# Splitting the weights on GpSimd: two instructions of 1024 columns in place of four of 512

## The chip, the cores and the metric

The kernel runs on one core of a Trainium2 chip. The metric is the time of the whole program on the device in microseconds; the median over several executions counts. In the profile, PE is TensorE's matmul side, DVE is VectorE, ACT is ScalarE, POOL is GpSimd and SP the queue that issues the weights' DMAs.

## The reference

Two networks in a row over one sequence of 512 tokens with 1024 features, all in float32. The first block joins multi-head latent attention and a bidirectional gated linear attention (GLA) behind one input projection, then a gated feed-forward network with a depthwise convolution over the grid. The second block has four layers: a mixer (recurrent, spatial gating, short convolution, recurrent again), each followed by an MLP of width 4096.

```python
def first_block(x, c, ctx, ...):
    mod = jax.nn.silu(c) @ w_ada + b_ada            # shifts, scales and gates from the condition
    h = modulate(rms_norm(x, norm1_g), sh1, sc1);  hc = modulate(rms_norm(ctx, norm1_g), sh1c, sc1c)
    x = x + gt1 * token_mixer(h, hc, ...)           # MLA attention and GLA
    x = x + gt2 * conv_ffn(modulate(rms_norm(x, norm2_g), sh2, sc2), ...)
    return rms_norm(x, final_g)

def second_block(x, ...):
    for i in range(4):
        x = x + mixer[i % 3](_rmsnorm(x, norm_mix_g[i]), ...)
        x = x + _sqrelu_mlp(_rmsnorm(x, norm_mlp_g[i]), mlp_w1[i], mlp_w2[i])
    return _rmsnorm(x, final_norm_g)
```

## The kernel before

Activations lie transposed, 128 features by 512 tokens in a tile, eight tiles for 1024 features. Every weight comes from HBM as a panel of eight 128x128 tiles (128 partitions by 1024 columns, 512 KB); there are 513 panels, and SP loads them into four slots `w_raw`. For accuracy each product is made of three matmuls: weights and activations are split into a high part, rounded to the matmul's format, and a low part, the difference. PE adds high by high, high by low and low by high (`mm`, line 1549), 24 matmuls of 512 columns in a panel.

GpSimd does nothing but split the weights. For a panel, `high(slot)` copies `w_raw` to `w_hi` with rounding (lines 1500 and 1501, the two halves of 512 columns), and `low_then_high` subtracts `w_hi` from `w_raw` into `w_lo` (lines 1511 and 1512, two halves again) and then makes `w_hi` of the next panel. Before `w_lo` of panel n it waits for three things: the next panel's landing, the high part, and `panel_used`, by which PE tells that it has begun panel n-2. So GpSimd runs up to three panels ahead of PE and each of its steps (low of n, high of n+1) is released by PE's first matmul of a panel. `panel_made` follows the second half of `w_lo` and is what PE and SP wait for.

The activations are split by ACT (the high part) and DVE (the low part, a subtraction of two SBUF tensors). Places that the prediction speaks of: `modulated` (lines 1094 and 1098) makes the first norm of `x` (`h_lo`) and of the context (`hc_lo`); `ada_product` (line 1117) multiplies a 128x1024 tile of `w_ada` by the condition vector and sums it, with 14 of these between the norm of `x` and that of the context; in the GLA `decays` (lines 1208, 1210 and 1213: a gated sum, a scan, a difference, each 768 columns wide) precede the transposes on PE; line 1301 adds the rotated half of a query head; line 1444 makes the last low part at the end of the first block, and line 1930 that at the end of each mixer and MLP (`feed_low`, behind the sums of squares of line 1923), always for tile 0 to 7, as PE's next product wants them in this order; line 1994 works on the recurrent mixer's input. Tiles named `acc`, `side` and `stat` are PSUM, all others that count here SBUF. The order of instructions on each engine is that of the program; nothing is scheduled.

Of the kernel before, what the change touches and what calls it, by code (L numbers as in the profile page):

```python
# [18 lines left out]
F32 = mybir.dt.float32  # L19
F32R = mybir.dt.float32r  # L20
ALU = mybir.AluOpType
# [3 lines left out]
P = 128  # L25
# [8 lines left out]
TP = 8  # L34
# [131 lines left out]
def build(nc, io, names, upto=None, start_x=False):  # L166

    n_panels = io["weights"].shape[0]
    with ExitStack() as whole:
        def sem(name):  # L170
            return whole.enter_context(nc.semaphore(name))

        def sb(name, shape, dt=F32):
            return whole.enter_context(nc.sbuf_tensor(name, shape, dt))
# [5 lines left out]
        w_raw = sb("w_raw", [P, SLOTS, TP * P])  # L180
        w_hi = sb("w_hi", [P, SLOTS, TP * P], F32R)
        w_lo = sb("w_lo", [P, SLOTS, TP * P], F32R)
# [41 lines left out]
        hi_made = sem("hi_made")  # L224
# [1241 lines left out]
        @block.sync  # L1466
        def _(sp):
            sp.dma_start(table[:, :], io["table"]).then_inc(const_in, 16)
            sp.dma_start(ones[:, :], io["ones"]).then_inc(const_in, 16)
            sp.dma_start(sgu_mask[:, :], io["sgu_mask"]).then_inc(const_in, 16)  # L1470
            if start_x:
                for k in range(KT):
                    sp.dma_start(x[:, k, :], io["x"][:, k, :]).then_inc(x_in, 16)
            if start_x:
                for slot in range(SLOTS):
                    load_panel(sp, slot, slot)
            if not start_x:
                first_block_sp(sp, load_panel)
            lead = SLOTS if start_x else LEAD
            turns = (n_panels - lead) // SLOTS  # L1480
            with sp.Fori(0, turns) as it:
                for slot in range(SLOTS):

                    sp.wait_ge(panel_made, it * SLOTS + (lead - SLOTS + slot + 1))
                    load_panel(sp, slot, it * SLOTS + (lead + slot))
            for n in range(lead + SLOTS * turns, n_panels):
                sp.wait_ge(panel_made, n - SLOTS + 1)
                load_panel(sp, n % SLOTS, n)
            for k in range(KT):
                sp.wait_ge(scaled, k + 1)  # L1490
                sp.dma_start(io["out"][:, k, :], x[:, k, :]).then_inc(result_out, 16)
            sp.wait_ge(result_out, 16 * KT)


        @block.gpsimd
        def _(pool):
            half = TP * P // 2

            def high(slot):
                pool.tensor_scalar(w_hi[:, slot, 0:half], w_raw[:, slot, 0:half], 1.0, 1.0, ALU.mult, ALU.mult)  # L1500
                pool.tensor_scalar(w_hi[:, slot, half:], w_raw[:, slot, half:], 1.0, 1.0, ALU.mult, ALU.mult).then_inc(hi_made, 1)  # L1501

            def low_then_high(slot, made, landed, used):

                after = (slot + 1) % SLOTS
                if landed is not None:
                    pool.wait_ge(raw_in[after], landed)
                if used is not None:
                    pool.wait_ge(panel_used, used)
                pool.wait_ge(hi_made, made)  # L1510
                pool.tensor_tensor(w_lo[:, slot, 0:half], w_raw[:, slot, 0:half], w_hi[:, slot, 0:half].bitcast(F32), ALU.subtract)  # L1511
                pool.tensor_tensor(w_lo[:, slot, half:], w_raw[:, slot, half:], w_hi[:, slot, half:].bitcast(F32),  # L1512
                                   ALU.subtract).then_inc(panel_made, 1)
                if landed is not None:
                    high(after)

            pool.wait_ge(raw_in[0], 16)
            high(0)
            for n in range(SLOTS - 1):
                low_then_high(n, n + 1, 16, None)  # L1520
            first = SLOTS - 1
            turns = (n_panels - 1 - first) // SLOTS
            with pool.Fori(0, turns) as it:
                for j in range(SLOTS):
                    low_then_high((first + j) % SLOTS, it * SLOTS + (first + j + 1), it * 16 + 32, it * SLOTS + (j + 1))
            for n in range(first + SLOTS * turns, n_panels):
                last = n == n_panels - 1
                low_then_high(n % SLOTS, n + 1, None if last else 16 * ((n + 1) // SLOTS + 1), None if last else n + 2 - SLOTS)
# [917 lines left out]
```

## Time and profile before

| | |
|---|---|
| median of 3 runs | 3238.98 us (3237.74 to 3240.68) |
| the profiled execution | 3237.74 us, its span 3235.8 us |
| PE busy | 3096.5 us, 96% of the span |
| GpSimd busy | 2073.4 us, 64%, 2056 instructions |
| DVE busy | 1455.3 us, 45% |
| ACT busy | 709.3 us, 22% |
| granted TensorE clock, mean | 0.979 |
| chain that ended last | PE 88%, DVE 8%, ACT 2% |

Busy time says which engine has the most work. The chain follows the last instruction back through what released it, so an engine off it has slack at that place. From 0 to 540 us (first block up to the merge of its two branches) PE has many gaps; after that it is busy nearly without one, apart from a few at the ends of stages. An instruction's duration in the profile runs from its issue to its end, so a wait inside the engine for something that no semaphore tells of is part of it.

### The profile page before, as it was taken

Reading aid. Unit: us, or ns where it says so; the run is one execution under the profiler, and the core shown is the slowest. Engines: PE = TensorE matmul, PEld = TensorE weight load, DVE = VectorE, ACT = ScalarE, POOL = GpSimd, SP = SyncE. Lnnn points to the kernel's source line nnn. Section 1 sums busy time; section 2 is a strip of 40 time slices with the busy share of each in tenths; the row PEclk is TensorE's granted clock in tenths of the full one; section 3 lists DMA queues with packets and bytes.
Section 4 is the critical chain, followed back from the end, with each engine's and each line's share of the span. In section 5 each row is a group of like instructions: output and inputs, shape, how many; then the busy total and the mean of one; then the engine's idle time right before and its main releaser. Section 6 shows DMA issues by size and latency. Waiting matters only on the chain.

```text
span 3235.8 us, 38599 instructions
## 1 busy us (share of the span) xinstructions
PE 3096.5 (96%) x13568; PEld 2485.2 (77%) x13568; DVE 1455.3 (45%) x1907; ACT 709.3 (22%) x1203; POOL 2073.4 (64%) x2056
## 2 busy tenths in 40 slices
PE   5878799989999999999999999999999999999998
PEld 3757646868888788888878888888888887888886
DVE  7866763247733774422225422255432226542222
ACT  3245463111000362200022200110211114421110
POOL 4623203756666677777767777777777776777774
PEclk8989899999999999999999999999999999999999
DMA  6701102223222232222232222222222222323221
GB/s 250 248 27 40 33 1 75 95 78 98 98 91 98 85 104 93 96 98 97 93 102 85 98 98 96 93 97 98 92 97 98 98 92 97 104 92 97 98 98 65
DMA packets 86009, 306.68 MB, mean 95 GB/s; under 512 B 9552, under 2 KB 10064, under 8 KB 85632
## 3 DMA queue, kind: packets, MB, share of 16 engines
q1 hardware_dynamic: 82512, 297.73, 27.5%
q10 hardware_dynamic: 3376, 7.24, 0.6%
q8 instruction: 87, 1.43, 0.2%
q14 instruction: 34, 0.28, 0.0%
HBM read 302.84 MB, written 2.10 MB: 94 GB/s over the span
## 4 chain that ended last, share of the span: by engine, by line
PE 88%; DVE 8%; ACT 2%; issue 1%; SPq 1%; DMA 1%; ACTq 0%; DVEq 0%
PE acc L1549 83%; PE side L735 1%; DVE rec_rec_x L1972 1%; PE acc L713 1%; DVE state L1265 1%; DVE ada_more L1117 1%; DMA xc<-in_ctx 1%; SPq L505 1%; PE acc L639 0%; PE acc L606 0%; PE acc L621 0%; PE side L1549 0%; PE stat L1612 0%; PE side L723 0%; DVE prob L1327 0%
## 5 line engine op out<-in xcount | busy, mean ns | idle before, releaser
L1511 POOL TENSOR_TENSOR w_lo<-w_raw,w_hi 128x512 fp32r<-128x512 f32 x513 | 672.2, 1310 | 1094.2 <-PE acc L1549 1067.9
L1549 PE MATMUL acc<-h_hi,w_hi 128*128 128x512 f32 x2224 | 878.7, 395 | 44.4 <-DVE state L1265 14.2
L1549 PE MATMUL acc<-h_lo,w_hi 128*128 128x512 f32 x2224 | 871.5, 392 | 0.0
L1549 PE MATMUL acc<-h_hi,w_lo 128*128 128x512 f32 x2224 | 871.5, 392 | 0.0
L1512 POOL TENSOR_TENSOR w_lo<-w_raw,w_hi 128x512 fp32r<-128x512 f32 x513 | 710.8, 1385 | 0.0
L1549 PEld LDWEIGHTS acc<-h_hi,w_hi 128*128 128x128 f32 x2224 | 420.5, 189 | 145.0 <-DVE state L1265 15.4
L1549 PEld LDWEIGHTS acc<-h_hi,w_lo 128*128 128x128 f32 x2224 | 420.9, 189 | 86.0
L1549 PEld LDWEIGHTS acc<-h_lo,w_hi 128*128 128x128 f32 x2224 | 420.9, 189 | 85.7 <-issue 1.7
L1500 POOL TENSOR_SCALAR w_hi<-w_raw 128x512 fp32r<-128x512 f32 x513 | 406.6, 793 | 37.3 <-DMA w_raw<-in_weights 37.3
L1941 DVE TENSOR_TENSOR x<-acc,x 128x512 f32 (+1 forms) x160 | 110.7, 692 | 671.1 <-PE acc L1549 671.0
L1549 PE MATMUL acc<-mlp_hid_hi,w_hi 128*128 128x512 f32 x1024 | 403.5, 394 | 0.0
L1549 PE MATMUL acc<-mlp_hid_hi,w_lo 128*128 128x512 f32 x1024 | 401.4, 392 | 0.0
L1549 PE MATMUL acc<-mlp_hid_lo,w_hi 128*128 128x512 f32 x1024 | 397.4, 388 | 0.0
L1501 POOL TENSOR_SCALAR w_hi<-w_raw 128x512 fp32r<-128x512 f32 x513 | 341.3, 665 | 0.0
L1869 ACT ACTIVATE mlp_hidden<-mlp_relu 128x512 f32<-128x512 f32 x128 | 81.0, 632 | 884.2 <-DVE mlp_relu L2171 884.2
L1948 DVE TENSOR_TENSOR mlp_hid_lo<-mlp_hidden,mlp_hid_hi 128x512 f32 (+1 forms) x128 | 171.9, 1343 | 178.6 <-ACT mlp_hid_hi L1870 178.6
L1549 PEld LDWEIGHTS acc<-mlp_hid_hi,w_lo 128*128 128x128 f32 x1024 | 192.2, 188 | 45.1
L1549 PEld LDWEIGHTS acc<-mlp_hid_lo,w_hi 128*128 128x128 f32 x1024 | 192.2, 188 | 43.0
L1549 PEld LDWEIGHTS acc<-mlp_hid_hi,w_hi 128*128 128x128 f32 x1024 | 192.5, 188 | 38.3
L2171 DVE SCALAR_TENSOR_TENSOR mlp_relu<-acc,rstd 128x512 f32<-128x512 f32 x128 | 88.6, 692 | 254.9 <-PE acc L1549 254.3
L1731 ACT ACTIVATE side<-x 128x512 f32<-128x512 f32 x64 | 38.5, 602 | 460.8 <-DVE x L1941 460.8
L1397 DVE SCALAR_TENSOR_TENSOR ff_conv<-acc,table,ff_conv 128x441 f32<-128x441 f32 (+2 forms) x176 | 122.4, 695 | 6.2
(341 smaller groups left out, 3612.1 us busy)
## 6 DMA issues: line engine op xcount, KB each, us to landing
w_raw<-in_weights SPq DMA_DIRECT2D x513, 512.0 KB, 3.3
ada<-in_ada SPq DMA_DIRECT2D x36, 512.0 KB, 5.8
ada_more<-in_ada SPq DMA_DIRECT2D x10, 512.0 KB, 18.4
x<-in_x ACTq DMA_DIRECT2D x16, 256.0 KB, 6.7
out<-x SPq DMA_DIRECT2D x8, 256.0 KB, 2.2
cvec<-in_cvec ACTq DMA_DIRECT2D x1, 1024.0 KB, 5.8
ada_n<-in_ada SPq DMA_DIRECT2D x2, 512.0 KB, 17.5
xc<-in_ctx SPq DMA_DIRECT2D x1, 1024.0 KB, 16.9
```

What stands on the lines that cost most here:

```text
L505: sp.dma_start(ada_slot[slot], io["ada"][m]).then_inc(ada_in[slot], 16)
L1397: ins = dve.scalar_tensor_tensor(out=out, in0=src[:, r0 + r:r1 + r, c0 + c:c1 + c], scalar=col("conv_w", FF1 * tap + j), in1=out, op0=ALU. ...
L1500: pool.tensor_scalar(w_hi[:, slot, 0:half], w_raw[:, slot, 0:half], 1.0, 1.0, ALU.mult, ALU.mult)
L1501: pool.tensor_scalar(w_hi[:, slot, half:], w_raw[:, slot, half:], 1.0, 1.0, ALU.mult, ALU.mult).then_inc(hi_made, 1)
L1511: pool.tensor_tensor(w_lo[:, slot, 0:half], w_raw[:, slot, 0:half], w_hi[:, slot, 0:half].bitcast(F32), ALU.subtract)
L1512: pool.tensor_tensor(w_lo[:, slot, half:], w_raw[:, slot, half:], w_hi[:, slot, half:].bitcast(F32), ALU.subtract).then_inc(panel_made, 1)
L1549: ins = pe.matmul(out, lhs, rhs, start=start, stop=stop, skip_group_check=group)
L1731: act.activation(squares(norm, k), x[:, k, :], ACT.Square).then_inc(squared, 1)
L1869: act.activation(M["hidden"][:, o % 4, :], M["relu"][:, o % 4, :], ACT.Square)
L1941: dve.tensor_tensor(tile, bank(o), tile, ALU.add).then_inc(out_taken[o % BANKS], 1)
L1948: dve.tensor_tensor(lo, whole_, hi.bitcast(F32), ALU.subtract).then_inc(made_sem, 1)
L2171: dve.scalar_tensor_tensor(out=M["relu"][:, o % 4, :], in0=bank(o), scalar=0.0, in1=rstd[:, :], op0=ALU.max, op1=ALU.mult).then_inc(out_ta ...
```

## The change

`high` and `low_then_high` make each part of a panel with one instruction of 1024 columns in place of two of 512. What is computed, the waits, the semaphore counts and the order are as they were.

```diff
         @block.gpsimd
         def _(pool):
-            half = TP * P // 2
-
             def high(slot):
-                pool.tensor_scalar(w_hi[:, slot, 0:half], w_raw[:, slot, 0:half], 1.0, 1.0, ALU.mult, ALU.mult)
-                pool.tensor_scalar(w_hi[:, slot, half:], w_raw[:, slot, half:], 1.0, 1.0, ALU.mult, ALU.mult).then_inc(hi_made, 1)
+                pool.tensor_scalar(w_hi[:, slot, :], w_raw[:, slot, :], 1.0, 1.0, ALU.mult, ALU.mult).then_inc(hi_made, 1)
...
                 pool.wait_ge(hi_made, made)
-                pool.tensor_tensor(w_lo[:, slot, 0:half], w_raw[:, slot, 0:half], w_hi[:, slot, 0:half].bitcast(F32), ALU.subtract)
-                pool.tensor_tensor(w_lo[:, slot, half:], w_raw[:, slot, half:], w_hi[:, slot, half:].bitcast(F32),
+                pool.tensor_tensor(w_lo[:, slot, :], w_raw[:, slot, :], w_hi[:, slot, :].bitcast(F32),
                                    ALU.subtract).then_inc(panel_made, 1)
```

GpSimd's queue in the loop over the panels, before (a panel and the start of the next; the names in brackets are the semaphores waited for):

```order
L1510 REGISTER_ALU [waits panel_used]
L1511 TENSOR_TENSOR w_lo<-w_raw,w_hi 128x512 [waits hi_made]
L1512 TENSOR_TENSOR w_lo<-w_raw,w_hi 128x512
L1500 TENSOR_SCALAR w_hi<-w_raw 128x512
L1501 TENSOR_SCALAR w_hi<-w_raw 128x512
L1509 REGISTER_ALU [waits raw_in1]
```

The same place after the change:

```order
L1507 REGISTER_ALU [waits panel_used]
L1508 TENSOR_TENSOR w_lo<-w_raw,w_hi 128x1024 [waits hi_made]
L1498 TENSOR_SCALAR w_hi<-w_raw 128x1024
L1506 REGISTER_ALU [waits raw_in1]
L1507 REGISTER_ALU [waits panel_used]
```

Four instructions have become two of twice the width between the same waits; the other engines' queues hold what they held.

## Rows read from the trace of the kernel before

**Rows 1.** The page's busy time of the engines.
```profile
PE 3096.5 (96%) x13568; PEld 2485.2 (77%) x13568; DVE 1455.3 (45%) x1907; ACT 709.3 (22%) x1203; POOL 2073.4 (64%) x2056
```
**Rows 2.** Page, costliest groups: busy us, mean ns, idle before and who ended it.
```profile
L1511 POOL TENSOR_TENSOR w_lo<-w_raw,w_hi 128x512 fp32r<-128x512 f32 x513 | 672.2, 1310 | 1094.2 <-PE acc L1549 1067.9
```
**Rows 3.** Timeline of DVE, 59 to 89 us: start, duration, instruction.
```profile
59.77 1.22 DVE L1117 SCALAR_TENSOR_TENSOR ada<-ada,cvec 128x1024 f32<-128x1024 f32 x1
...
69.63 2.30 DVE L1117 SCALAR_TENSOR_TENSOR ada_more<-ada_more,cvec 128x1024 f32<-128x1024 f32 x1
...
74.10 1.62 DVE L1117 SCALAR_TENSOR_TENSOR ada_more<-ada_more,cvec 128x1024 f32<-128x1024 f32 x1
...
83.21 1.62 DVE L1117 SCALAR_TENSOR_TENSOR ada_more<-ada_more,cvec 128x1024 f32<-128x1024 f32 x1
...
87.28 1.75 DVE L1087 RECIPROCAL rstd<-root 128x256 f32<-128x256 f32 x1
```
**Rows 4.** Timeline of POOL, 60 to 93 us.
```profile
61.30 1.98 POOL L1511 TENSOR_TENSOR w_lo<-w_raw,w_hi 128x512 fp32r<-128x512 f32 x1 [7.15 <-PE acc L1549]
...
70.81 2.27 POOL L1512 TENSOR_TENSOR w_lo<-w_raw,w_hi 128x512 fp32r<-128x512 f32 x1
73.06 1.59 POOL L1500 TENSOR_SCALAR w_hi<-w_raw 128x512 fp32r<-128x512 f32 x1
...
91.87 0.78 POOL L1501 TENSOR_SCALAR w_hi<-w_raw 128x512 fp32r<-128x512 f32 x1
```
**Rows 5.** Timeline of PE, where the context's products begin; in brackets the idle time before.
```profile
99.70 0.76 PE L1549 MATMUL acc<-h_hi,w_hi 128*128 128x512 f32 x1 [11.58 <-ACT gq L845]
```
**Rows 6.** Timelines of POOL and DVE in the GLA, 192 to 199 us.
```profile
192.78 1.29 POOL L1511 TENSOR_TENSOR w_lo<-w_raw,w_hi 128x512 fp32r<-128x512 f32 x1 [20.25 <-PE acc L1549]
...
193.82 1.07 DVE L1208 SCALAR_TENSOR_TENSOR zb<-zb,ln 128x768 f32<-128x768 f32 x1
194.92 2.73 DVE L1210 TENSOR_TENSOR_SCAN b_cum<-reset,zb 128x768 f32<-128x768 f32 x1
197.69 1.19 DVE L1213 TENSOR_TENSOR kd<-b_cum 128x768 f32<-128x768 f32 x1
```
**Rows 7.** Timelines of POOL and DVE in the GLA, 296 to 299 us.
```profile
296.48 1.56 POOL L1511 TENSOR_TENSOR w_lo<-w_raw,w_hi 128x512 fp32r<-128x512 f32 x1 [4.50 <-PE acc L1549]
...
297.00 1.86 DVE L1213 TENSOR_TENSOR kd<-b_cum 128x768 f32<-128x768 f32 x1
```
**Rows 8.** Timelines of POOL and DVE, query heads, 367 to 372 us.
```profile
367.86 1.83 POOL L1511 TENSOR_TENSOR w_lo<-w_raw,w_hi 128x512 fp32r<-128x512 f32 x1 [1.01 <-PE acc L1549]
...
370.03 1.46 DVE L1301 TENSOR_TENSOR q_t<-q_t,square 32x512 f32<-32x512 f32 x1
```
**Rows 9.** Timelines of DVE, POOL and PE, end of the first block.
```profile
1073.00 1.53 DVE L1444 SCALAR_TENSOR_TENSOR h_lo<-x,gain,h_hi 128x512 fp32r<-128x512 f32 x1
...
1077.40 0.75 DVE L1444 SCALAR_TENSOR_TENSOR h_lo<-x,gain,h_hi 128x512 fp32r<-128x512 f32 x1
...
1078.22 1.30 POOL L1511 TENSOR_TENSOR w_lo<-w_raw,w_hi 128x512 fp32r<-128x512 f32 x1 [1.37 <-PE acc L1549]
...
1084.78 0.79 PE L1549 MATMUL acc<-h_hi,w_hi 128*128 128x512 f32 x1 [1.86 <-DVE h_lo L1444]
```
**Rows 10.** Timelines of POOL and DVE in the first recurrent mixer.
```profile
1147.53 1.30 POOL L1511 TENSOR_TENSOR w_lo<-w_raw,w_hi 128x512 fp32r<-128x512 f32 x1 [1.66 <-PE acc L1549]
...
1148.25 1.13 DVE L1994 SCALAR_TENSOR_TENSOR rec_rec_u<-rec_rec_sq,rec_rec_u 128x512 f32<-128x512 f32 x1
```
**Rows 11.** Timelines of POOL, DVE and PE, from the recurrent mixer to its MLP.
```profile
1289.39 1.29 POOL L1511 TENSOR_TENSOR w_lo<-w_raw,w_hi 128x512 fp32r<-128x512 f32 x1 [1.70 <-PE acc L1549]
1290.23 1.00 DVE L1930 SCALAR_TENSOR_TENSOR h_lo<-x,table,h_hi 128x512 fp32r<-128x512 f32 x1
...
1291.76 1.18 DVE L1930 SCALAR_TENSOR_TENSOR h_lo<-x,table,h_hi 128x512 fp32r<-128x512 f32 x1
...
1294.32 0.59 PE L1612 MATMUL stat<-square_sum,ones 128*128 128x512 f32 x1
```

## The prediction, made before the changed kernel had run

> **What bounds the kernel now.** I read the busy times first: PE works 96% of the span and POOL 64% [rows 1]. The waits come next: no wait of PE is put down to POOL anywhere, while POOL's splitting of the low part has stood idle for 1094.2 us, 1067.9 of them until PE began another panel [rows 2]. So the weights are always ready in time, and a shorter split by itself is worth nothing. Then I read the chain that ended last: PE, but for the first 540 us and the ends of stages, where it runs over DVE. So the question is whether the change touches DVE. It does: the timelines of DVE and POOL side by side show that they stop each other.
>
> **How they stop each other.** The DVE product of 1024 columns takes 1.22 us at 59.77, with POOL idle; at 69.63 it takes 2.30 and at 74.10 it takes 1.62 [rows 3]. POOL's instruction at 70.81 takes 2.27 us, to 73.08, and that at 73.06 takes 1.59 [rows 4]. Laid on one axis they take turns: DVE's of 69.63 gets nothing until POOL's neighbour of 70.81 ends, then needs 1.12 and ends at 71.93; POOL's of 70.81 has waited for that and needs 73.08 - 71.93 = 1.15; DVE's next comes after it. DVE's two durations differ by 0.68, so a high part of 512 columns holds what they share for about 1.15 - 0.68 = 0.48. So it is one instruction of the one, whole, then one of the other. It strikes DVE instructions with two SBUF inputs (1117, 1208 to 1213, 1301, 1444, 1930, the squared form of 1994), and not those with one input in PSUM or the reciprocals. The Trainium skill says this too (page "SBUF — State Buffer", section "SBUF: two separate sides"): the pair of ports that both use is an exclusive lock, held for the whole instruction by whoever starts first. By that rule, the trace agrees.
>
> **The change, part by part.** It removes 2 x 513 POOL instructions; SP's, PE's, ACT's and DVE's queues stay as they are, and no wait is added. The work is as large: I take the holding at twice a half's, 2.3 us for the low part and 0.97 for the high one, and a low part that starts unhindered as 2.45 us from its start (1.29 twice, less some 0.1 for one start). No row shows a 1024-column instruction on POOL. The bounds are the half's own 1.29 us (nothing for the second half) and 2.6 (nothing saved); the row of the half doubled is the nearest. The saving, about 0.2 us a panel on POOL, is worth 0: it lies in POOL's 1067.9 us of waiting for PE. What moves the time is that a DVE instruction which comes while POOL holds the lock now waits for the rest of 2.3 us and not of 1.15. Place by place along the chain:
>
> A. From 59.77 DVE runs 14 products up to 84.83 [rows 3], 25.1 us of which they need 14 x 1.15 = 16.0. In the same time POOL does three panels, each 4 turns: 4 x 1.07 for DVE and 3.3 of its own, 7.5 us. With two turns a panel takes 2 x 1.07 + 3.3 = 5.4 us, which is PE's own pace for a panel. So POOL is stopped later by PE and brings all of the five panels that lay between 61.30 and 92.65 [rows 4] into the 14 products: 5 x 3.3 = 16.5 us of waiting, less 0.08 at each of ten turns, against 9.1. That is 6.6 later, and 0.9 more comes from the first norm just ahead, where DVE and ACT hand tiles to each other and DVE meets the same turns (an estimate: three panels are split there). Some 3.5 come back, because the small instructions, the reciprocal at 87.28 [rows 3] and the first context tiles now run undisturbed. PE waits for the end of this at 99.70, 11.58 us long [rows 5], so it is late in full: **+4.0**. Bounds: 0, if the same five panels already stood wholly in its way, and +7.5, if nothing comes back.
>
> B. In the GLA, at 192.78 a low part now holds until 195.2; DVE's 1208 ends at 196.1 and not 194.89, the high part goes to 197.05, the scan ends at 198.7 and 1213, now undisturbed, at 199.65 against 198.88 [rows 6]: +0.8. At 296.48 POOL waits for the scan, then holds 2.3: 1213 ends 1.2 late [rows 7]. At 252 us one high part ends sooner: -0.2. Three more such places (220, 266, 313 us) have slack of over 2 us, and three panels lie under a reciprocal. Together **+1.8**, between 0 and +3.5.
>
> C. In the query heads DVE runs without a pause and PE waits for its end. Two panels fall in: the first costs 1.0, and behind the second, at 367.86, the addition of 368.6 to 370.9 and the next, which took 1.46 at 370.03 [rows 8], end 1.5 late in all: **+1.5**, between 0 and +2.4.
>
> D. At the end of the first block DVE is again without a pause. The `h_lo` of 1073.00 ends 1.2 late. The next, at 1077.40, took 0.75 because it came just before POOL's low part of 1078.22; 1.2 later it comes just behind it and waits until 1080.65, so it is 3.1 late. The last frees PE at 1084.78 [rows 9]: **+3.0**, between 0 and +3.2.
>
> E. In both recurrent mixers the squared form of 1994 meets a low part that began 0.7 before (1147.53 and 1148.25 [rows 10]) and ends 1.2 late, in a run of DVE without a pause at whose end PE waits: 2 x 1.2 = **+2.3**, between 0 and +2.6.
>
> F. From mixer to MLP and on: the low part that starts at 1289.39 holds until 1291.85, so `h_lo` of tile 6 ends at 1292.45 and not 1291.23; the high part then takes its turn to 1293.4, and tile 7's ends at 1294.0 and not 1292.94. PE's statistics matmul of 1294.32 stands three matmuls of 0.23 behind the first that needs tile 7 [rows 11], so that one was due at 1293.64: it is 0.35 late. The same rows recur, to a hundredth or two, at six stage ends: 6 x 0.35 = **+2.1**, and two like them at the merge and the short convolution add 0.2. Between 0 and +4.5, since half a us more in the holding counts six times.
>
> Sum: 4.0 + 1.8 + 1.5 + 3.0 + 2.3 + 2.3 = +14.9. The rest of the 3096.5 us [rows 1] is PE's own and doesn't move: in the MLPs DVE's `mlp_hid_lo` will take up to a us longer, under 5.5 us of matmuls to each. The profiled execution took 3237.7, 1.2 under the median, so 3252.6 against it and 3254 against the median; I say **3253**.
>
> The skill also gives (page "GPSIMD Engine Reference", section 2.1) a dispatch in software for each instruction and about 2.5 cycles an element for two inputs. An estimate from that with the page's 1.2 GHz is 2.1 us for 1024 columns, against my 2.3 from the trace; by it the sum would be lower by some 2 us.
>
> **The rivals.**
> 1. *No measurable change* (within 0.2%, 6.5 us, which is about what a measurement of this kernel tells from none). The holding per panel is the same 3.3 us; if DVE's long waits at one place are repaid by clear ones at the next, only C and E stay, with half of A: +5, 3244. For it: POOL finishes a panel sooner, and A gives some back. Against it: in D to F a run of DVE ends soon behind the longer wait, with nothing left to repay it. Chance 0.19.
> 2. *Faster.* If a wide instruction runs its columns at a better rate, as it pays its start once, the holding shrinks: at 2.0 instead of 2.3 us the five panels in A hold 1.5 us less; and with turns halved, where DVE has one instruction between two of POOL, it waits once and not twice. It decides below 1.6 us, where all terms from B on turn negative: -7, 3232. Nothing in the rows speaks for so steep a gain: on DVE 1024 columns cost 1.12 in the lock. Chance 0.04.
> 3. *Much slower.* New gaps of PE of 2 to 5 us, above all at D and E, make the clock fall to 1.2 GHz for a while, as it has behind 99.70, where the first matmul takes 0.76 [rows 5]. A short fall costs as much again as the gap: three of them and F at its upper bound make +23, 3262. Chance 0.15.
> The forecast has 0.62. Cases over +6.5 us hold 0.77.
>
> Range: the bounds of the terms don't all fall together; 3241 to 3263 leaves out most of rival 2, part of rival 1 and the tail beyond rival 3. Slower 0.77, same 0.19, faster 0.04.
>
> **What will show it.** POOL has 1026 instructions fewer and its two groups take some 2.4 and 1.1 us on the mean or a little more. DVE's products at 60 to 90 us show 3.4 us and 2.0 where they meet POOL, and 1.22 elsewhere; the idle time at 99.70 grows by about 3 to 4 us; the gap behind line 1444 grows from 1.86 to near 5; those behind the recurrent mixers' long runs grow from 1.9 to 3; six new gaps of 0.3 to 0.4 appear at the stage ends. No wait of PE on POOL. It would be wrong if DVE's longest product stays at 2.3 us (the turn isn't a whole instruction), or if these instructions wait as described and PE's gaps don't grow.

## The result: 0.5% slower, 15.8 us, and near the forecast

The changed kernel took 3254.75 us in the median of 5 runs (3254.29 to 3257.84), the kernel before 3238.98 (3236.07 to 3241.47) beside it: a ratio of 1.0051, 95% interval 1.0036 to 1.0066. The forecast was 3253, with 3241 to 3263 as its range. The profiled execution took 3257.22 us with a span of 3255.4, that is 19.6 more span than before, so it was one of the slower ones on its side and the one of before one of the faster ones on its own; where I add up terms below, they add up to 19.6 and not to 15.8. PE's own busy time is 10.2 us more than in [rows 1], with the same matmuls: only half of the 19.6 stands in its idle time. How much of the rest is time at the lower clock is worked out at the end.

The page of the changed kernel, busy times and POOL's two groups (busy us, mean ns of one | idle before them, and who ended it):

```profile
PE 3106.7 (95%) x13568; PEld 2489.8 (76%) x13568; DVE 1509.9 (46%) x1907; ACT 709.0 (22%) x1203; POOL 1875.7 (58%) x1030
...
L1508 POOL TENSOR_TENSOR w_lo<-w_raw,w_hi 128x1024 fp32r<-128x1024 f32 x513 | 1243.2, 2423 | 1311.1 <-PE acc L1545 1264.4
...
L1498 POOL TENSOR_SCALAR w_hi<-w_raw 128x1024 fp32r<-128x1024 f32 x513 | 650.2, 1267 | 37.2 <-DMA w_raw<-in_weights 37.2
```

POOL has 1026 instructions fewer and is busy 197.7 us less than in [rows 1]; the splitting waits for PE longer than in [rows 2], 1264.4 us. DVE, which the change doesn't touch, is busy 54.6 us more. That is time spent inside its instructions, waiting for the ports that it shares with POOL, as the rows below show place by place. POOL, which got work taken off, was not on the chain that ended last; DVE, which pays, stands in some places right before PE.

Where the condition's products are made, the timeline of DVE (start, duration, instruction), which answers to [rows 3]:

```profile
59.70 1.22 DVE L1117 SCALAR_TENSOR_TENSOR ada<-ada,cvec 128x1024 f32<-128x1024 f32 x1
...
61.99 3.41 DVE L1117 SCALAR_TENSOR_TENSOR ada<-ada,cvec 128x1024 f32<-128x1024 f32 x1
...
65.33 2.05 DVE L1117 SCALAR_TENSOR_TENSOR ada<-ada,cvec 128x1024 f32<-128x1024 f32 x1
...
67.31 3.40 DVE L1117 SCALAR_TENSOR_TENSOR ada_more<-ada_more,cvec 128x1024 f32<-128x1024 f32 x1
```

and POOL's, which answers to [rows 4] (idle time before in brackets):

```profile
61.22 3.10 POOL L1508 TENSOR_TENSOR w_lo<-w_raw,w_hi 128x1024 fp32r<-128x1024 f32 x1 [10.01 <-PE acc L1545]
64.29 2.02 POOL L1498 TENSOR_SCALAR w_hi<-w_raw 128x1024 fp32r<-128x1024 f32 x1
66.65 2.99 POOL L1508 TENSOR_TENSOR w_lo<-w_raw,w_hi 128x1024 fp32r<-128x1024 f32 x1 [0.34 <-PE acc L1545]
```

Both alternate, whole instruction by whole instruction, as forecast: 3.41 where DVE waits behind a low part, 2.05 behind a high one, five such pairs in the 14 products. From start to start a free product takes 60.85 - 59.70 = 1.15, the two of a pair 3.34 and 1.98. So a whole low part holds the ports for 2.19 us and a whole high one for 0.83.

PE waits for the end of this, in the row that answers to [rows 5]:

```profile
102.40 0.77 PE L1545 MATMUL acc<-h_hi,w_hi 128*128 128x512 f32 x1 [14.38 <-ACT gq L845]
```

To see where the rest comes from, the matmuls of both traces can be counted through: PE's order is the same, so the start of the k-th matmul before the change can be subtracted from the start of the k-th after it. This is how much later (us) some of them start than before, with one column for each kernel (the columns of the experiments are used further down):

| matmul at (before, us) | what lies just ahead | changed | again | low whole | high whole | early whole | late whole | low quarters | low short |
|---|---|---|---|---|---|---|---|---|---|
| 85.0 | | -0.1 | -0.1 | 0.0 | -0.1 | 0.1 | -0.3 | 1.9 | -3.3 |
| 101.1 | condition's products | 2.7 | 2.7 | 2.1 | 1.6 | 2.9 | -0.1 | -2.0 | -8.6 |
| 352.5 | GLA | 5.8 | 7.0 | 6.1 | 1.3 | 3.0 | -1.1 | -7.1 | -11.7 |
| 381.3 | query heads | 8.2 | 7.8 | 7.0 | 3.2 | 5.2 | 0.3 | -6.8 | -11.3 |
| 545.1 | attention | 8.4 | 7.4 | 9.4 | 5.6 | 7.2 | 2.7 | -7.0 | -10.8 |
| 1040.1 | first MLP | 8.7 | 7.9 | 9.2 | 5.0 | 7.6 | 3.3 | -6.9 | -11.4 |
| 1085.4 | end of first block | 11.6 | 10.8 | 12.1 | 5.1 | 7.3 | 6.2 | -7.4 | -12.0 |
| 1119.2 | | 13.4 | 10.7 | 12.2 | 5.4 | 7.6 | 9.1 | -7.1 | -13.3 |
| 1170.1 | first recurrent mixer | 14.5 | 13.0 | 13.1 | 3.9 | 6.0 | 11.5 | -7.1 | -14.9 |
| 1297.0 | a stage end | 14.8 | 13.5 | 13.6 | 3.9 | 6.0 | 11.8 | -7.1 | -14.9 |
| 2675.1 | four more, short conv | 16.6 | 15.3 | 17.2 | 3.8 | 6.0 | 13.6 | -7.1 | -14.9 |
| 2702.0 | | 18.2 | 16.9 | 18.8 | 3.8 | 6.0 | 15.2 | -7.1 | -14.9 |
| 2750.2 | second recurrent mixer | 19.3 | 18.0 | 19.9 | 3.8 | 6.0 | 16.3 | -7.2 | -15.0 |
| 3223.1 | last stage end | 19.6 | 18.3 | 20.4 | 3.8 | 6.0 | 16.6 | -7.1 | -14.9 |

Each column is one profiled execution, and some of these lie off their kernel's median: that of low short by -8.7 us, that of early whole by -4.0. So the last line of a column is not the cost that the medians give.

Four places of the changed kernel, each in the timelines of its engines. In the GLA (POOL, then DVE), answering to [rows 6]:

```profile
195.10 2.38 POOL L1508 TENSOR_TENSOR w_lo<-w_raw,w_hi 128x1024 fp32r<-128x1024 f32 x1 [20.54 <-PE acc L1545]
...
196.14 2.16 DVE L1208 SCALAR_TENSOR_TENSOR zb<-zb,ln 128x768 f32<-128x768 f32 x1
198.34 2.47 DVE L1210 TENSOR_TENSOR_SCAN b_cum<-reset,zb 128x768 f32<-128x768 f32 x1
200.84 0.96 DVE L1213 TENSOR_TENSOR kd<-b_cum 128x768 f32<-128x768 f32 x1
```

L1208 starts 2.32 us later than before, and L1213 ends at 201.80 against 198.88, 2.92 later: this place gave 0.6. At the end of the first block (DVE, POOL, PE), answering to [rows 9]:

```profile
1081.53 2.77 DVE L1444 SCALAR_TENSOR_TENSOR h_lo<-x,gain,h_hi 128x512 fp32r<-128x512 f32 x1
...
1087.18 2.66 DVE L1444 SCALAR_TENSOR_TENSOR h_lo<-x,gain,h_hi 128x512 fp32r<-128x512 f32 x1
...
1081.36 2.40 POOL L1508 TENSOR_TENSOR w_lo<-w_raw,w_hi 128x1024 fp32r<-128x1024 f32 x1 [1.79 <-PE acc L1545]
...
1086.89 2.40 POOL L1508 TENSOR_TENSOR w_lo<-w_raw,w_hi 128x1024 fp32r<-128x1024 f32 x1 [1.67 <-PE acc L1545]
...
1093.52 0.79 PE L1545 MATMUL acc<-h_hi,w_hi 128*128 128x512 f32 x1 [2.66 <-DVE h_lo L1444]
...
1096.36 0.80 PE L1545 MATMUL acc<-h_hi,w_hi 128*128 128x512 f32 x1 [1.19 <-DVE h_lo L1444]
```

Two `h_lo` in a row now stand behind a whole low part (2.77 and 2.66 us, where they took 1.53 and 0.75); the one gap of 1.86 us has become two, 3.85 together. In the first recurrent mixer (POOL, DVE, PE), answering to [rows 10]:

```profile
1160.93 2.41 POOL L1508 TENSOR_TENSOR w_lo<-w_raw,w_hi 128x1024 fp32r<-128x1024 f32 x1 [1.95 <-PE acc L1545]
...
1161.63 2.26 DVE L1990 SCALAR_TENSOR_TENSOR rec_rec_u<-rec_rec_sq,rec_rec_u 128x512 f32<-128x512 f32 x1
...
1177.15 0.51 PE L1545 MATMUL acc<-rec_rec_hi,w_hi 128*128 128x512 f32 x1 [2.73 <-DVE rec_rec_lo L1975]
```

The squared form takes 2.26 us and not 1.13. And at the first stage end (POOL, DVE, PE), answering to [rows 11]:

```profile
1303.90 2.41 POOL L1508 TENSOR_TENSOR w_lo<-w_raw,w_hi 128x1024 fp32r<-128x1024 f32 x1 [1.99 <-PE acc L1545]
...
1304.74 2.11 DVE L1926 SCALAR_TENSOR_TENSOR h_lo<-x,table,h_hi 128x512 fp32r<-128x512 f32 x1
...
1307.38 0.93 DVE L1926 SCALAR_TENSOR_TENSOR h_lo<-x,table,h_hi 128x512 fp32r<-128x512 f32 x1
...
1307.92 0.39 PE L1545 MATMUL acc<-h_hi,w_lo 128*128 128x512 f32 x1
1308.36 0.50 PE L1545 MATMUL acc<-h_hi,w_hi 128*128 128x512 f32 x1
```

Tile 7's `h_lo` ends at 1308.31, and the matmul behind it starts 0.44 after its neighbour where the others follow after 0.23. Such a gap is too short for the list of waits; only the counting shows it, as +0.3 at each of six stage ends.

### The profile page after: what moved, and what is told of

It is laid out like the page before. It is cut to its first block, busy times and chain, and to the rows that moved or that the text cites. A ratio compares the mean times of both kernels' runs of the same rounds, so it can differ in the third digit from the quotient of the medians.

```text
span 3255.4 us, 37573 instructions
## 1 busy us (share of the span) xinstructions
PE 3106.7 (95%) x13568; PEld 2489.8 (76%) x13568; DVE 1509.9 (46%) x1907; ACT 709.0 (22%) x1203; POOL 1875.7 (58%) x1030
## 3 DMA queue, kind: packets, MB, share of 16 engines
q1 hardware_dynamic: 82512, 297.73, 27.3%
## 4 chain that ended last, share of the span: by engine, by line
PE 87%; DVE 9%; ACT 2%; issue 1%; SPq 1%; DMA 1%; ACTq 0%; DVEq 0%
PE acc L1545 81%; PE side L735 1%; DVE ada_more L1117 1%; DVE rec_rec_x L1968 1%; PE acc L713 1%; DVE state L1265 1%; DMA xc<-in_ctx 1%; SPq L505 1%; PE acc L639 0%; PE acc L621 0%; PE acc L606 0%; PE side L1545 0%; PE side L723 0%; DVE prob L1327 0%; PE stat L1608 0%
## 5 line engine op out<-in xcount | busy, mean ns | idle before, releaser
L1508 POOL TENSOR_TENSOR w_lo<-w_raw,w_hi 128x1024 fp32r<-128x1024 f32 x513 | 1243.2, 2423 | 1311.1 <-PE acc L1545 1264.4
L1498 POOL TENSOR_SCALAR w_hi<-w_raw 128x1024 fp32r<-128x1024 f32 x513 | 650.2, 1267 | 37.2 <-DMA w_raw<-in_weights 37.2
L1545 PEld LDWEIGHTS acc<-h_hi,w_hi 128*128 128x128 f32 x2224 | 420.5, 189 | 152.8 <-DVE state L1265 15.2
L1944 DVE TENSOR_TENSOR mlp_hid_lo<-mlp_hidden,mlp_hid_hi 128x512 f32 (+1 forms) x128 | 156.3, 1221 | 178.6 <-ACT mlp_hid_hi L1866 178.6
L1545 PE MATMUL acc<-rec_rec_hi,w_hi 128*128 128x512 f32 x264 | 106.4, 403 | 9.1 <-DVE rec_rec_lo L1975 9.1
L1545 PE MATMUL acc<-rec_rec_hi,w_lo 128*128 128x512 f32 x264 | 105.3, 399 | 0.0
## 6 DMA issues: line engine op xcount, KB each, us to landing
ada_more<-in_ada SPq DMA_DIRECT2D x10, 512.0 KB, 18.3
```

The lines of the kernel that those rows point to most:

```text
L1498: pool.tensor_scalar(w_hi[:, slot, :], w_raw[:, slot, :], 1.0, 1.0, ALU.mult, ALU.mult).then_inc(hi_made, 1)
L1508: pool.tensor_tensor(w_lo[:, slot, :], w_raw[:, slot, :], w_hi[:, slot, :].bitcast(F32), ALU.subtract).then_inc(panel_made, 1)
L1545: ins = pe.matmul(out, lhs, rhs, start=start, stop=stop, skip_group_check=group)
L1944: dve.tensor_tensor(lo, whole_, hi.bitcast(F32), ALU.subtract).then_inc(made_sem, 1)
```

## The experiments

The theory: a POOL instruction holds the ports that it shares with DVE from its start to its end, so what the change costs is the longer single hold, put on those DVE instructions that PE waits for. The rivals: the width or the number of POOL's instructions matters in itself (their starts, their rate), or the order of POOL's instructions; or the loss is all from the early part of the kernel, where DVE has most to do. In all kernels but whole again (the changed kernel itself) and low short, POOL's splitting is written with these two loops, and the table gives the number of instructions for one panel. The short diffs further down are against these loops with `HI, LO = 2, 2`, which is what the kernel before does; remarks in them are mine:

```diff
+            for c in parts(HI):      # 1024 columns in HI equal pieces
+                ins = pool.tensor_scalar(w_hi[:, slot, c], w_raw[:, slot, c], 1.0, 1.0, ALU.mult, ALU.mult)
+            ins.then_inc(hi_made, 1)
...
+            for c in parts(LO):
+                ins = pool.tensor_tensor(w_lo[:, slot, c], w_raw[:, slot, c], w_hi[:, slot, c].bitcast(F32), ALU.subtract)
+            ins.then_inc(panel_made, 1)
```

| kernel | HI | LO | median us (lowest to highest, runs) | before | ratio, 95% |
|---|---|---|---|---|---|
| low whole | 2 | 1 | 3258.82 (3257.87 to 3264.31, 5) | 3238.58 | 1.0064, 1.0050 to 1.0078 |
| high whole | 1 | 2 | 3242.29 (3237.75 to 3246.62, 11) | 3238.58 | 1.0011, 1.0002 to 1.0020 |
| early whole | 1, then 2 | 1, then 2 | 3247.60 (3241.95 to 3251.82, 11) | 3238.58 | 1.0026, 1.0017 to 1.0035 |
| late whole | 2, then 1 | 2, then 1 | 3254.06 (3250.86 to 3255.80, 5) | 3238.58 | 1.0042, 1.0028 to 1.0055 |
| whole again | 1 | 1 | 3254.75 (3254.47 to 3263.53, 5) | 3238.83 | 1.0055, 1.0041 to 1.0069 |
| unrolled halves | 2 | 2 | 3240.07 (3237.08 to 3245.15, 11) | 3238.83 | 1.0006, 0.9997 to 1.0015 |
| low quarters | 2 | 4 | 3230.75 (3229.65 to 3236.94, 9) | 3238.83 | 0.9978, 0.9968 to 0.9988 |
| low short | 1 | 1, with one input (below) | 3231.40 (3222.67 to 3232.63, 11) | 3238.83 | 0.9975, 0.9966 to 0.9984 |
| quarters | 4 | 4 | 3230.17 (3226.28 to 3240.57, 8) | 3240.48 | 0.9971, 0.9960 to 0.9981 |
| low eighths | 2 | 8 | 3234.13 (3231.14 to 3237.39, 11) | 3240.48 | 0.9981, 0.9972 to 0.9989 |

The ratio compares with executions of the kernel before made beside it, whose median stands under "before".

**Each half of the change alone.**

```diff
-            HI, LO = 2, 2
+            HI, LO = 2, 1      # low whole
```

> Only the low part w_lo is made by one GpSimd instruction of 1024 columns; the high part stays in two of 512. Theory (a GpSimd instruction and a VectorE instruction with two SBUF inputs shut each other out, each for its whole length, so that the wait grows with the longest instruction): the places after the first 60 us hang on the low part's hold of 2.3 us, so most of the 16 us come: the `h_lo` run at the end of the first block +3, the squared form of the recurrent mixers +2, the six stage ends +2, the gated attention and the query heads +4, the condition's products less than the whole change (three turns a panel and not two), +1 to +2; with the clock's falls 10 to 14 us slower than before. Rival (it is the number of turns or of instructions, not the length): half the removed instructions, so half the loss, +8, and the same for the high part alone.

```diff
-            HI, LO = 2, 2
+            HI, LO = 1, 2      # high whole
```

> Only the high part w_hi is made by one GpSimd instruction of 1024 columns; the low part stays in two of 512. Theory (the wait grows with the longest instruction in the lock): the longest hold stays the low half's 1.15 us, the high part's grows from 0.48 to 0.97; +0 to +3 us, with no new gap at the six stage ends and the gap before PE's statistics unchanged at the end of the first block (1.86 us within 0.5). Rival (number of instructions or turns): +8, as for the low part alone.

Low whole cost 20.2 us, where 10 to 14 were expected, and at least as much as the whole change; high whole 3.7, just over its range of 0 to 3. The low part's instruction carries the loss. Two rows, DVE's products in the two kernels, show why the halves differ: where both have a low part ahead of the product, it takes

```profile
62.08 3.41 DVE L1117 SCALAR_TENSOR_TENSOR ada<-ada,cvec 128x1024 f32<-128x1024 f32 x1
```

in low whole and

```profile
62.00 2.30 DVE L1117 SCALAR_TENSOR_TENSOR ada<-ada,cvec 128x1024 f32<-128x1024 f32 x1
```

in high whole, as in [rows 3]. In the table of delays high whole has no step at the end of the first block nor at any stage end; low whole has both, and its stage ends cost 0.45 to 0.5 and not 0.3. The halves add up to 23.9 us and the change to 16. What was wrong in the expectation is that each half was given a cost of its own: whether a DVE instruction falls just ahead of a long hold or just behind it depends on the sum of all delays before it. That this makes up the excess is argued and not shown.

**The change in one part of the kernel alone.** The first 31 panels are written out, and the loop does the rest:

```diff
-            for n in range(SLOTS - 1):
-                low_then_high(n, n + 1, 16, None)
+            for n in range(FIRST):     # FIRST = 31
+                low_then_high(n % SLOTS, n + 1, 16 * ((n + 1) // SLOTS + 1), n + 2 - SLOTS if n + 2 > SLOTS else None, EARLY)
```

> Whole instructions for the first 31 panels (to the end of attention), halves behind them. Theory: what the changed kernel lost up to there, +8.5 in its trace, and nothing after: 8 us slower than before (6 to 10), and the delay of PE's matmuls against before stays flat from 550 us on. Rival (the losses are one thing spread over the whole run, such as a slower clock or memory, in proportion to the panels): 31 of 513 panels, +1.

> Halves for the first 31 panels, whole instructions behind them. Theory: the rest of the loss, +7.5 against before (6 to 11 with the clock's falls): +3 at the end of the first block, +0.9 in each recurrent mixer, +0.33 at each of six stage ends and about that at the merge and the short convolution. Early and late together should give the whole change's +16. Rival (in proportion to the panels): +15.

Early whole cost 9.0 us as expected (its trace shows 6.0), late whole 15.5 against 7.5 expected (6 to 11): a miss. The column of late whole says where. End of the first block +2.9, stage ends and the second mixer the same steps as in the changed kernel: these are as worked out, some 8 us. But 1.4 came in the query heads (-1.1 to 0.3), before any whole instruction ran, because DVE's turns there (timeline of DVE, late whole)

```profile
362.48 1.69 DVE L1301 TENSOR_TENSOR q_t<-q_t,square 32x512 f32<-32x512 f32 x1
...
367.83 1.73 DVE L1301 TENSOR_TENSOR q_t<-q_t,square 32x512 f32<-32x512 f32 x1
```

came just behind POOL's, by chance of when they arrive; 2.4 came in the attention (0.3 to 2.7), with 5.3 us more at half clock; and 3.0 at 1119 and 1.6 at 2702 are falls of the clock, told below. The control of the next paragraph, which has halves throughout, gains the same 1.4 and 2.4 in these two places, so they don't come from whole instructions. Early and late add up to 24.5 us and the change to 16: the parts don't add.

**The change once more, and the control for the writing out.**

> The changed kernel once more, on the same chip as the next three, because the loss of the first 31 panels (+9.0 us) and that of the rest (+15.5) measured apart add up to 24.5 and not to the 16 of the whole. If places on the chain add up and the excess is the clock and the order of arrivals at the lock, this repeats +16 within 3. If it comes out at +20 or more, it was the chip that differed.

> Control for the two kernels that treat the first 31 panels apart: halves everywhere, as before, but with GpSimd's first 31 panels written out instead of looped. If writing them out is free, 0 within 1 us. Rival for the excess of 8 us: the writing out itself costs, some +4 here, counted twice in the sum of the two parts.

The change came back at +15.9 us. Written out with halves, the first 31 panels cost 1.2 us, which can't be told from nothing; so early and late whole may be read as they stand. But the delays of its matmuls against the kernel before, with the same instructions in the same order, wandered between -2.4 (at 258 us) and +1.9 (at 541) and ended at +0.3. That is the noise in which any single term of 1 or 2 us before 1100 us is to be read.

**Shorter holds than before.**

```diff
-            HI, LO = 2, 2
+            HI, LO = 2, 4      # low quarters
```

> The other way: the low part in four instructions of 256 columns, the high part in two halves as before. Theory (the wait grows with the length held): the longest hold falls from 1.15 us to about 0.6. At the end of the first block the two waits of a low half shrink, -0.8; in each recurrent mixer -0.3; the query heads -0.4, the scans and products of the gated attention -0.5; the six stage ends had slack, 0. In the condition's products six turns a panel cost more of the panels' pace and put less of the holding ahead of PE's wait: -1. Together -3 us, between -6 and +2. Rival (each instruction or turn costs, whatever its length): 1026 instructions more, so slower, and by as much as their removal should have won.

It took 8.1 us off, beyond the expected range of -6 to +2, and beats both kernels. Page and timelines of DVE, POOL and PE:

```profile
L1517 POOL TENSOR_TENSOR w_lo<-w_raw,w_hi 128x256 fp32r<-128x256 f32 x2052 | 1595.6, 810 | 926.7 <-PE acc L1554 906.9
```

```profile
61.84 1.75 DVE L1117 SCALAR_TENSOR_TENSOR ada<-ada,cvec 128x1024 f32<-128x1024 f32 x1
...
61.36 6.18 POOL L1517 TENSOR_TENSOR w_lo<-w_raw,w_hi 128x256 fp32r<-128x256 f32 x4 [4.54 <-PE acc L1554]
...
84.36 0.47 PE L1554 MATMUL acc<-h_hi,w_hi 128*128 128x512 f32 x1 [1.14 <-POOL w_lo L1517]
```

POOL is busier, 1595.6 us for the low part against 1243.2, and the kernel is faster. DVE waits 1.69 - 1.15 = 0.54 from start to start behind a low part (61.84 to 63.53); but POOL, too, has to wait for a product before each of its six turns, so that it gets through only two panels and a quarter of one from 61.36 to 82.14, where the changed kernel got through four. The 14 products take from 59.55 to 81.56, 22.0 us, against 31.2 in the changed kernel and 25.1 before. The price is in the row of 84.36: PE now waits for POOL. Nothing of the gain comes after 352 us (-7.1 from there to the end), where the expectation had put about half of it. And of the 7.1 only 2.0 stand by 101 us, behind the products. The other 5.1 come in the GLA, where the trace has 8.6 us less at half clock; there the control with halves came out 2.3 us early too. How much of the 5.1 is owed to shorter holds stays open.

**A short hold in wide instructions.** This kernel leaves out the low part of the weights (but for 8 columns, zeros stand in its place), so as to have a low part with one input:

```diff
-                pool.tensor_tensor(w_lo[:, slot, :], w_raw[:, slot, :], w_hi[:, slot, :].bitcast(F32),
-                                   ALU.subtract).then_inc(panel_made, 1)
+                pool.tensor_tensor(w_lo[:, slot, 0:8], w_raw[:, slot, 0:8], w_hi[:, slot, 0:8].bitcast(F32), ALU.subtract)
+                pool.tensor_scalar(w_lo[:, slot, 8:], w_raw[:, slot, 8:], 0.0, 1.0, ALU.mult, ALU.mult).then_inc(panel_made, 1)
```

> The same whole 1024-column instructions as the changed kernel, but the low part is made by an instruction with one input (w_raw times zero; 8 columns of the subtraction stand ahead of it), so it holds some 1.0 us and not 2.3. It leaves out the low part of the weights: w_lo is zero, PE's work is the same. Theory: the longest hold is now below the low half's 1.15, so the loss of 16 us is gone: at the end of the first block PE's wait is at most the 1.86 us of before, none at the stage ends; -4 us against before, between -8 and +1. Rival (the width of the instruction, or two turns in place of four, and not the time held): still +16.

It ran 7.4 us faster than before, 23.4 faster than the change whose widths it has. Its page (POOL's instruction of the low part) and the timelines of DVE and POOL:

```profile
L1509 POOL TENSOR_SCALAR w_lo<-w_raw 128x1016 fp32r<-128x1016 f32 x513 | 541.8, 1056 | 0.0
```

```profile
59.95 2.05 DVE L1117 SCALAR_TENSOR_TENSOR ada<-ada,cvec 128x1024 f32<-128x1024 f32 x1
...
63.46 0.58 POOL L1508 TENSOR_TENSOR w_lo<-w_raw,w_hi 128x8 fp32r<-128x8 f32 x1 [0.55 <-PE acc L1545]
64.01 2.02 POOL L1509 TENSOR_SCALAR w_lo<-w_raw 128x1016 fp32r<-128x1016 f32 x1
```

The longest product is 2.05 us. PE has one gap of 1.87 us at the end of the first block, as before, and no step at the stage ends. POOL's instructions are as wide as in the changed kernel and in the same order, with one more of 8 columns in each panel; what is shorter is the time for which the low part holds. That rules out the first rival and the order. The rival of an early loss only fell with late whole. The size of the gain is less clear: the trace shown is the fastest of 11 executions, and in it the products already start 2.0 us earlier (57.65 against 59.70 in the changed kernel).

**How short is best.**

> Both parts of the weights in four instructions of 256 columns (the low part alone in four took 8.1 us off). If the time held in one turn is all that counts, a high part of 0.25 us a turn instead of 0.48 takes 1 to 3 us more off: about 3229, -9 to -11 against the kernel before. The other side: with the low part in four PE already waited 1.4 us for POOL in the query heads and the GLA (the panel's turns are ten times 1.1 us beside a DVE that runs without a pause), and eight turns a panel make that wait 5 us or more: 3233 to 3238, that is slower than the low part alone in four. I take -8, between -12 and -2.

> High part in two instructions, low part in eight of 128 columns. A turn of the low part then holds some 0.35 us and not 0.63. If only the time held counts, 3 to 5 us go beside the low part in four: -11 to -13 against the kernel before. The rival: ten turns a panel, with 1.1 us for DVE in each, make a panel last 15 us while DVE runs its products from 60 to 80 us, against PE's 5.4 us; POOL brings fewer than two panels in that time where PE uses four, the reserve of four slots is used up, and PE waits for POOL: 5 to 10 us at 75 to 85 us, again in the GLA and the query heads. By that it is slower than the low part in four by 5 to 20: -3 to +12. I take +3, since POOL's wait shows already in the run before.

Quarters for both parts took 10.3 us off (interval 6 to 13), low eighths 6.4 (interval 4 to 9). Neither can be told from low quarters (8.1, interval 4 to 10), so which of the three is best stays open. But the expected cost of too many turns is there in low eighths (timelines of DVE, POOL and PE):

```profile
65.61 1.47 DVE L1117 SCALAR_TENSOR_TENSOR ada_more<-ada_more,cvec 128x1024 f32<-128x1024 f32 x1
...
64.70 11.09 POOL L1517 TENSOR_TENSOR w_lo<-w_raw,w_hi 128x128 fp32r<-128x128 f32 x8
...
75.84 0.79 PE L1554 MATMUL acc<-h_hi,w_hi 128*128 128x512 f32 x1 [6.94 <-POOL w_lo L1517]
```

A product of DVE is down to 1.47 us, but one panel's low part takes 11.09, and PE stands for 6.94 us waiting for it. All waits of PE for POOL in the three kernels, from the table of waits (total us, times, longest), first low quarters, then quarters, then low eighths:

```profile
PE acc L1554 <- POOL w_lo L1517: 1.4, 2, 1.1
```

```profile
PE acc L1554 <- POOL w_lo L1517: 6.2, 4, 3.6
```

```profile
PE acc L1554 <- POOL w_lo L1517: 12.8, 4, 6.9
```

The expectation for the eighths, +3 with bounds -3 and +12, was too dark, and 6.4 us off lies outside it: the wait of 12.8 us came, but part of it lies in time that PE would else have waited for the context's products (its matmul at 85.0 starts 6.6 us later than before, that at 101.1 starts 1.4 earlier).

## Why the forecast was right, step by step

**How they stop each other**: as read from [rows 3, 4]. By turns, a whole instruction at a time; the Trainium skill's rule of an exclusive lock held for the whole instruction (page "SBUF — State Buffer", section "SBUF: two separate sides") is borne out by 3.41, 2.30, 1.75 and 1.47 us for the same product behind a low part of 1024, 512, 256 and 128 columns. **The holdings**, forecast 2.3 and 0.97 us, measured 2.19 and 0.83: each a little too high. The free instructions, forecast 2.45, take 2.41 on POOL (1160.93). The estimate of 2.1 us from the Trainium skill's figures (page "GPSIMD Engine Reference", section 2.1) lay as near to the measured hold as mine.

**A, forecast +4.0, measured +2.7.** Five pairs, each with 3.34 + 1.98 - 2 x 1.15 = 3.02 of waiting, put the end of the products at 90.94 against 84.83: +6.1 and not +6.6. And 3.4 came back behind them, where I had 3.5. What failed is the 0.9 for the first norm: the products start at 59.70 against 59.77, so it was not later at all.

**B, forecast +1.8, measured +3.1** (2.7 to 5.8). The place of [rows 6] gave 0.6 and not 0.8, and that of [rows 7] 1.1 and not 1.2 (DVE, then PE):

```profile
298.90 2.97 DVE L1213 TENSOR_TENSOR kd<-b_cum 128x768 f32<-128x768 f32 x1
...
306.74 0.44 PE L615 MATMUL acc<-identity,kd 128*128 128x128 f32 x2 [3.38 <-DVE kd L1221]
```

L1213 takes 2.97 us and not 1.86, and PE's gap behind it, 2.26 before, is 3.38. So the waits come to 1.7 of the 1.8. The other 1.4 are nearly all clock, as a net: -1.4 in the stretches before and between these places and +2.8 from 303.7 to 352.5 us, where PE has no new gap but 27.3 us at half clock and not 17.1.

**C, forecast +1.5, measured +2.4.** A low part and the addition of L1301 start together, at 374.64 and 374.65 (POOL, DVE, PE):

```profile
374.64 2.36 POOL L1508 TENSOR_TENSOR w_lo<-w_raw,w_hi 128x1024 fp32r<-128x1024 f32 x1 [2.74 <-PE acc L1545]
...
374.65 2.89 DVE L1301 TENSOR_TENSOR q_t<-q_t,square 32x512 f32<-32x512 f32 x1
...
377.60 0.50 PE L1545 MATMUL acc<-om_hi,w_hi 128*128 128x512 f32 x1 [2.02 <-DVE q_t L1301]
```

I had let the addition come 0.7 us behind the start of the low part (368.6 against 367.86). Before the change, and again in the repetition, the two started together as well, but there the addition went first (DVE before; POOL, then DVE in the repetition):

```profile
367.86 0.68 DVE L1301 TENSOR_TENSOR q_t<-q_t,square 32x512 f32<-32x512 f32 x1
```

```profile
375.82 2.95 POOL L1508 TENSOR_TENSOR w_lo<-w_raw,w_hi 128x1024 fp32r<-128x1024 f32 x1 [2.75 <-PE acc L1545]
...
375.82 0.68 DVE L1301 TENSOR_TENSOR q_t<-q_t,square 32x512 f32<-32x512 f32 x1
```

So with starts within a hundredth of a us of each other either can be first, and 2.2 us hang on it; in the repetition C measures 0.8 (7.0 to 7.8). That my +1.5 lies between the two is luck.

**D, forecast +3.0, measured +2.9**, by the very two instructions. **E, forecast +2.3, measured +2.2** in two steps of 1.1, the gap ahead 0.9 longer in each. **F with the merge and the short convolution, forecast +2.3, measured +2.6**: 0.3 at each of six stage ends, 0.35 at the short convolution, 0.2 at the merge and 0.2 in the spatial gating (1753 us before), which I had not seen.

**The rest, +3.6, is the clock too**, the mechanism of my third rival, but at other places than I gave it: behind the gaps at D and in the first recurrent mixer the clock fell before the change as well. It is a net +0.2 in the attention, 1.8 at 1119 and 1.6 at 2702 us. Here is what the rows show. A matmul of the first recurrent mixer, before the change and after it:

```profile
1115.43 0.50 PE L1549 MATMUL acc<-rec_rec_hi,w_hi 128*128 128x512 f32 x1 [1.82 <-DVE rec_rec_lo L1979]
```

```profile
1127.22 0.66 PE L1545 MATMUL acc<-rec_rec_hi,w_hi 128*128 128x512 f32 x1 [1.82 <-DVE rec_rec_lo L1975]
```

and the stretches of the changed kernel behind it (columns: us; busy time and count of PE, its weight loads, DVE, ACT, POOL; the granted clock; DMA):

```profile
1127.40:1130.80 3.40, 3.40 (x9) 2.65 (x10) 1.15 (x2) 2.88 (x4) 0.00 (x0) 0.50 0.26 102
1130.80:1134.20 3.40, 3.40 (x17) 2.78 (x16) 0.50 (x2) 1.35 (x2) 1.98 (x1) 1.00 0.00 0
```

The gap ahead is the same 1.82 us in both. Behind it the clock stayed at 2.4 GHz in the one and fell to 1.2 GHz in the other, 9 matmuls in 3.4 us and not 17; it cost 1.6. But this fall isn't the change's: of all twelve traces it is missing in four, the kernel before, the repetition, low whole and low short, and it is there in the other eight, the control with halves among them. The same gap of 1.82 us lies ahead of 2702 in all twelve; behind it the clock fell in the changed kernel, its repetition, low whole and late whole, and in none of the other eight. The change doesn't make either gap; it moves the time at which they come. The Trainium skill says in "TensorE: Matmul & The Clock Gate", Part 1, that the gate watches activity in a rhythm of its own that no kernel starts; a fall that depends on when the same gap comes agrees with it, and no run here tests it further. In all, the trace has 155 us at half clock against 134 before, and the repetition 152.

So the mechanism was right, and the waits too: without the clock's 3.6 and the 1.4 in B the profile has 14.6, of 14.9 forecast. That the sums agree so closely is partly luck, since A measured 1.3 less than forecast and C 0.9 more. A, D, E and F recur in the repetition (2.7, 2.9, steps of 0.9 and 1.1, six of 0.3); B and C don't (4.3 and 0.8 there), for there the wait behind a whole low part falls on L1213 at 252 us and not at 299. The medians are 15.8 apart, 1 us from the sum, and that is luck in part as well: the forecast put nothing on the clock, and the two profiled executions show some 5 us of it.

Of the signs that I had named, the long products (3.41 and 2.05), POOL's means (2.42 and 1.27), the steps at six stage ends and the missing wait of PE's matmuls on POOL are there; the gaps grew by less than I had said, 2.8 and not 3 to 4 us at 102.40, 3.85 in two and not near 5 in one behind line 1444, 2.73 and not 3 in the recurrent mixers.

Left open: what share of the clock's time the medians carry, why the fall at 2702 us came in just the four traces with a whole subtraction there, and why low whole alone cost as much as the change or more (its interval and the change's overlap).

## What to carry to other kernels

Where two engines take turns by whole instructions, the one taxes the other by the length of one instruction, and its total busy time doesn't tell the cost. So try shorter instructions, where that engine has time to spare and its neighbour stands before the bound engine, and stop where the bound engine begins to wait for it; look for that at the place where the neighbour runs without a pause. And a saving of starts on an engine that waits most of the time is to be priced at nothing before anything else is.

## What the runs showed of the hardware that I had not expected

- More and shorter instructions on POOL cost it 352 us of busy time (1595.6 against 1243.2, with its waits for DVE in it) and made the kernel 24 us faster than the changed one: each turn that POOL must wait for also slows POOL, and in the 14 products that left DVE 22.0 us and not 31.2.
- The clock fell behind a PE gap of 1.82 us in some traces and not in others: at 1115 us (in the time of the kernel before) in eight of twelve, at 2697 us in four of twelve, with the same length of gap each time. A fall there cost 1.6 us.
- Where a DVE and a POOL instruction start within 0.01 us of each other, either can be first: the same addition took 2.89 us in one execution of the changed kernel and 0.68 in the other.
- Twice the same instructions in the same order (unrolled halves) drifted apart by up to 2.4 us on the way and came together again. Steps of the delay say something only where they recur, as at the stage ends.
